# The order in DRAM of the expert weights between two stages of a mixture-of-experts kernel

## What is computed

```python
eidx, gates = ...            # 8 heads x 16 choices out of 128*128 experts, per token
act = gelu(einsum('td,thkd->thk', hb, u_tab[eidx]))
out = einsum('thk,thkd->td', gates * act, v_tab[eidx])
```

## Time and profile before

| | |
|---|---|
| median of 3 runs | 2834.89 us (2833.07 to 2837.03) |
| profiled execution, its own time | 2837.42 us |
| its span | 2835.6 us |
| TensorE clock granted, mean | 0.971 of full speed |
| `weigh` | about 1950 to 2259 us |
| `combine` | 2259 us to the end |
| DMA packets, all queues | 192715, 535.04 MB |

### The profile page before, as it was taken

The page is one execution under the profiler, slowest core; times in us unless marked ns, Lnnn a source line. Parts: engine busy times, 40 slices in busy tenths (PEclk is TensorE's granted clock), DMA queues, the critical chain, the costliest instruction groups (busy, mean ns, idle before and its releaser), DMA issues. The chain is left out here.

```text
span 2835.6 us, 37682 instructions
## 1 busy us (share of the span) xinstructions
PE 2651.7 (94%) x13701; PEld 2227.5 (79%) x13701; DVE 1932.5 (68%) x3068; ACT 1044.9 (37%) x1667; POOL 1293.0 (46%) x607
## 2 busy tenths in 40 slices
PE   8999999799999999889688999999999889999997
PEld 6888877555778887668476899998999868888776
DVE  5445232687754444465755177778999789999999
ACT  4222321355232223222122133335666534444343
POOL 4444442111344444333133457773222267777774
PEclk9999999899999999999798999999999989999999
DMA  5444342112334443222002355557999999999995
GB/s 194 148 148 129 105 152 60 46 59 90 89 119 141 141 154 111 81 90 74 15 7 73 92 150 159 167 166 286 398 377 380 368 346 372 376 375 376 376 372 185
DMA packets 192715, 535.04 MB, mean 189 GB/s; under 512 B 20192, under 2 KB 99296, under 8 KB 172512
## 3 DMA queue, kind: packets, MB, share of 16 engines
q1 hardware_dynamic: 94496, 305.11, 33.5%
q0 software_dynamic: 18432, 134.23, 11.9%
q10 hardware_dynamic: 79680, 94.38, 9.5%
HBM read 478.09 MB, written 55.57 MB: 188 GB/s over the span
## 5 line engine op out<-in xcount | busy, mean ns | idle before, releaser
L352 POOL TENSOR_TENSOR ring_low<-ring,ring_high 128x1024 fp32r<-128x1024 f32 x323 | 801.5, 2485 | 1065.9 <-ACT ring_high L312 1061.9
L403 PE MATMUL ps<-u_high,ring_high 128*128 128x512 f32 (+1 forms) x1728 | 659.3, 382 | 51.9 <-DVE u_low L659 16.9
L404 PE MATMUL ps<-u_low,ring_high 128*128 128x512 f32 (+1 forms) x1728 | 650.4, 376 | 0.0
L405 PE MATMUL ps<-u_high,ring_low 128*128 128x512 f32 (+1 forms) x1728 | 650.3, 376 | 0.0
L312 ACT ACTIVATE ring_high<-ring 128x1024 fp32r<-128x1024 f32 x354 | 373.4, 1055 | 566.0 <-PE ps L405 527.4
L403 PEld LDWEIGHTS ps<-u_high,ring_high 128*128 128x128 f32 x1728 | 328.3, 190 | 114.3 <-issue 40.7
L404 PEld LDWEIGHTS ps<-u_low,ring_high 128*128 128x128 f32 x1728 | 328.7, 190 | 48.8 <-issue 2.0
L405 PEld LDWEIGHTS ps<-u_high,ring_low 128*128 128x128 f32 x1728 | 328.3, 190 | 49.0
L2490 POOL DMA_INDIRECT fetched_rows<-in_peer_uv,fetch_index x128 | 166.2, 1299 | 311.8 <-DVE ps L2510 274.1
L352 POOL TENSOR_TENSOR ring_low_more<-ring,ring_high_more 128x1024 fp32r<-128x1024 f32 x96 | 245.1, 2565 | 32.1 <-ACT ring_high_more L312 31.5
L3088 DVE TENSOR_TENSOR expert_coef_low<-expert_product,expert_coef_high 128x384 fp32r<-128x384 f32 x128 | 216.4, 1691 | 9.3 <-ACT expert_coef_high L3049 9.2
(11 more groups left out here) (439 smaller groups left out, 4865.1 us busy)
## 6 DMA issues: line engine op xcount, KB each, us to landing
ring<-in_peer_u SPq DMA_DIRECT2D x128, 512.0 KB
ring<-in_peer_uv SPq DMA_DIRECT2D x128, 512.0 KB
ring<-in_ffn_gu SPq DMA_DIRECT2D x88, 512.0 KB
ada_weights<-in_ada_w SPq DMA_DIRECT2D x48, 512.0 KB, 4.2
ring<-in_ffn_down SPq DMA_DIRECT2D x48, 512.0 KB
expert_acts<-kept_acts ACTq DMA_DIRECT2D x128, 192.0 KB, 5.0
expert_weights<-weight_stage ACTq DMA_DIRECT2D x24, 1024.0 KB, 10.0
group_acts<-expert_acts ACTq DMA_DIRECT2D x14, 1536.0 KB, 17.8
```

Of the source, the lines that this page charges most:

```text
L352: pool.tensor_tensor(k.lows[p], k.ring[:, s], k.highs[p].bitcast(F32), ALU.subtract)\
L403: pe.matmul(out, k.highs[p][:, w], high, start=first, stop=False)
L404: pe.matmul(out, k.highs[p][:, w], low, start=False, stop=False)
L405: last = pe.matmul(out, k.lows[p][:, w], high, start=False, stop=final)
```

## The change

The intermediate tensor `expert_weights` gets another order in DRAM. Before, it is [block of 16 tokens, partition, expert tile, token]; after, it is [group of eight tiles, partition, block, tile and token]. With it, a store of a block, whose source is one run of 8 KB in each partition, goes to 16 runs of 512 bytes (one in each group; from one group to the next it is 128 x 24 x 512 bytes = 1.5 MiB), 2048 pieces in all instead of 128. The load of a whole group with all 24 blocks, before 24 runs of 512 bytes in each partition (3072 pieces), is one run of 12 KB in each partition (128); for group 1, with 23 blocks, 2944 pieces become 128 runs of 11.5 KB. The two loads of parts of group 0 (two tiles: 128 bytes for each block; six tiles: 384 bytes) keep their 2944 pieces each. Nothing else is changed: the same DMAs, in the same order, with the same waits and the same bytes.

```diff
@@ -2887,8 +2887,8 @@ (weigh, ACT: the store of a block)
                     if part == 1:
                         act.wait_ge(taken[b].sem, taken[b].at(h // 2 + 1))
-                        act.dma_start(k.dram["expert_weights"][h // 2],
-                                      stage[:, slot].rearrange("p e t -> p (e t)")).then_inc(x.staged[slot].sem, 16)
+                        act.dma_start(k.dram["expert_weights"][:, :, h // 2].rearrange("g p n -> p g n"),
+                                      stage[:, slot].rearrange("p (g e) t -> p g (e t)", e=8)).then_inc(x.staged[slot].sem, 16)
@@ -2990,7 +2990,7 @@ (combine: the load of a group)
         def load_weights(eng, g, blocks, lo, hi, landed):
             eng.dma_start(weights[:, g % 2, 0:blocks, lo * WT:hi * WT],
-                          k.dram["expert_weights"][0:blocks, :, 8 * g + lo:8 * g + hi].rearrange("b p e t -> p b (e t)"))\
+                          k.dram["expert_weights"][g, :, 0:blocks, lo * WT:hi * WT])\
                .then_inc(landed.sem, 16)
@@ -3162,7 +3162,7 @@ (build)
-        weights = nc.dram_tensor("expert_weights", (NB, P, P, WT), F32, kind="Internal").ap()
+        weights = nc.dram_tensor("expert_weights", (V_ITERS, P, NB, 8 * WT), F32, kind="Internal").ap()
```

## The result

| | before | after |
|---|---|---|
| median on the same chip | 2833.98 us (2832.33 to 2837.03, 4 runs) | 2858.17 us (2856.26 to 2863.81, 4 runs) |
| ratio | | 1.0084, 95% interval 1.0072 to 1.0096 |
| span of the profiled execution | 2835.6 us | 2854.4 us |
| `weigh`, from DVE's first one-hot to ACT's last activations | 317.5 us | 340.3 us |
| from there to the first product of group 1 | 48.1 us | 47.1 us |

The change costs 24 us. The forecast was 2838 us, a change too small to be measured; 24 us are four times the 5.7 that the prediction calls the least that can be told from none, and 2858 is above its range, which ended at 2856. The table places the loss: 22.8 us in `weigh`, -1.0 in the passage, +0.5 in what follows. (These make 22.3; the profiled spans lie only 18.8 apart because the stages ahead of `weigh`, which the change doesn't touch, ended 3.6 us earlier in that execution.)

What follows compares the result with a forecast made beforehand. Engines were taken to set the pace of weigh and combine, with the DMA close behind. Terms of +4 (ACT's queue), -1 (passage) and 0 (throughput) gave +3 us: a median of 2838 us, forecast's own range 2831 to 2841, overall 2830 to 2856.

Steps and rivals of the forecast that it cites:

- the term of ACT's queue: In weigh, ACT's next DMA is held behind a 2048-piece store: 0.5 us an iteration, +4 us in eight.
- the room that the sum relied on: In weigh, buffers behind ACT's queue absorb 2.4 us of backlog: slots refilled 13.4 us after a store that lands in 9.8.
- Rival (c): In weigh, ACT is held at every store, 24 times 1 to 2 us felt by PE and DVE: about 2862 us; chance 0.12.
- What a piece costs: DMA price: 512-byte pieces move at 294 GB/s, 27.9 ns each, so a megabyte costs 1.4 times that in long pieces.
- weigh's throughput at 0: In weigh, short stores raise DMA demand to 40.4 us against 40.1 an iteration; taken as 0, bounds 0 and +8 us.
- Rival (b): In weigh, DMA becomes the bound if a store's piece costs over 28 ns (33 estimated): 2847 us; chance 0.25.
- (d): In weigh, stores with pieces 1.5 MiB apart run at half rate, +88 us: 2923 us; chance 0.03.
- Combine: In combine, long loads cut DMA work from 32.6 to 31.0 us a group, but nothing waits for DMA: gain 0.
- The passage: Between weigh and combine, group 1's weights load faster but the last stores land later: net -1 us, bounds -4 and +5.
- Rival (e): Long load runs are cut into 512-byte pieces anyway while stores are short, the passage losing its gain: 2841 us; chance 0.03.
- (f): Faster: weigh holds its pace without any hold, and the passage gains its 2 to 4 us and 3 to 4 more: 2828 us; chance 0.11.

Runs made afterwards that it cites:

- e13: The kernel after, with each weight store cut into two halves of eight groups, one issued by ACT and one by SP: 2839.91 us, 1.0012 of before.
- e4: The kernel after, with the 24 weight stores issued by SP between its ring loads instead of by ACT: 2841.89 us, 1.0017 of before.
- e1: The kernel after, with weight stores in long 8 KB runs as before and loads still long (values permuted): 2836.78 us, 0.9996 of before.
- e7: The kernel before, with group 0 loaded in one piece and four ring tiles loaded ahead of group 1 in the passage: 2827.55 us, 0.9975 of before.
- e11: The kernel before, with one more wait: DVE waits at tile 12 of combine for the weights of group 2: 2835.17 us, 0.9999 of before.
- e14: e7 with long stores and long loads of the weights (values permuted): 2831.66 us, 0.9982 of before.
- e5: The kernel after, with the tensor laid out by sixteen tiles, so a store has 1024 pieces of 1 KB: 2847.46 us, 1.0039 of before.
- e10: The kernel after, with weigh's 64 stores of activations issued by SP, the weight stores staying on ACT: 2850.34 us, 1.0047 of before.

## Why the prediction was wrong

**The step that failed is the term of ACT's queue**: +4 us taken, some 20 us measured (22.8 in weigh less the 2.4 that e13 leaves). That is within the term's own bounds, 0 and 3 us an iteration (24 in all); the forecast stood near the lower one. The mechanism was the one described there: a hold of the DMA issued behind a store, until some of its pieces have gone. Four things in the sizing were off.

- When the store starts. "Alone, 35 pieces take 1.0 us and start a little over 1 us after the issue: no hold." No row gave that start. By the packet records it is 3.6 us (median of 24 stores), and ACT's next issue comes 1.4 to 2.7 us behind the store, before it has started in 21 of 24 cases; 36 us of the holds are this.
- How long the other queues keep taking turns. I let one gather and one or two ring tiles (8 packets an engine for each) stand against 35 pieces (3 to 5 us). In the first hold 52 packets of q10 went by, and 32 of the gathers and 28 of the ring took turns with them, 14.35 us in all. The sign of it was in the trace of before (rows below). I had read landing times from 1982 us on the earlier trace rows, that is without the first iteration, which alone lost 13.0 of the 22.8 us.
- What stands behind the held issue. I looked at the next copy of activations, ahead of which ACT idles for 2.72 us. Behind two of three stores it is the copy of a half out of PSUM that stands there (63.0 us of waits at L2885, 25.4 at L2743), and PE's next products into these banks wait for it (26.0 us, 12.7 before).
- How often. "The first two stores of an iteration I cost at nothing; if that cover is gone, they cost the same again": 23 of 24 stores held the issue behind them, not one in three. In six of the eight iterations (all but the second and the fourth) the time grew by 0.8 us or more.

What the second point left unread, the DMA of the kernel before from 1942 to 1982 us: the gathers' queue (42.4% over all of 1942 to 2222), and the landing of the three long stores of that iteration.

```profile
q0 software_dynamic: 1234, 8.96, 53.9%
...
expert_weights<-weight_stage ACTq DMA_DIRECT2D x3, 1024.0 KB, 18.0
```

These stores landed in 18.0 us where later ones do in 9.8: the room that the sum relied on was used up there already.

Of the 112 us of holds a fifth reached the end; a sum over holds would have been as wrong as my 4 us.

**Rival (c)**, at 0.12, was what happened: +24 to +48 by its text, +24.2 measured, by ACT and PE that feel the holds. Only it isn't spread over all stores alike, as that text has it: more than half falls in one iteration.

**What a piece costs** was wrong for the stores. The 27.9 ns are a load's. Where ACT's queue is alone in after, 1981 to 1982.5 us, stored pieces of 512 bytes go by like this:

```profile
DMA packets 1019, 0.52 MB, mean 347 GB/s; under 512 B 1, under 2 KB 1019, under 8 KB 1019
```

These are 1.5 us x 16 / 1019 = 23.6 ns each; two more such stretches of after (2049.8 to 2051, 1990.8 to 1992.6) show 346 and 349 GB/s, and one of e4 on SP's queue (2011 to 2012) 347. The loads of the kernel before stay at 292 (2361.2 to 2362.4). So, with the 410 GB/s of the prediction for long pieces, a stored megabyte in 512-byte pieces costs 410 / 347 = 1.18 times what it costs in long ones, not 1.4. The prediction set the 1.17 of the Trainium skill (DMA: Bandwidth & Descriptors, section Why small descriptors are slow) aside because a trace of loads disagreed with it; the trace of the stores agrees. With 347 the three stores of an iteration cost 1.4 us more, not 3.0, and the demand is 38.8 us in 40.1: under the pace of the engines, not 0.3 over. So **weigh's throughput at 0** came out right (within the 2.4 us that e13 leaves), though the cover for it, room in the buffers, wasn't needed. Rival (b) needed more than 28 ns and is out, and so is (d), which needed twice the price. In (d) the reading of a rule went too far: the Trainium skill (DMA: Bandwidth & Descriptors, section Latency and other measured facts) gives the loss by the pitch from one partition's row to the next. That pitch is 8 KB in the loads of before and 12 KB in the stores of after, and the 1 and 1.5 MiB lie between the pieces of one partition, so neither kernel tests the rule.

That q10 alone falls behind, as the prediction argued, is so, and no slot was waited for. But ACT was held by its queue before any buffer was full, and the argument looked at the buffers.

**Combine** held: 3062 packets in a group (some 3040 forecast), 33.69 us against 33.65, and e1 shows the same without the disturbed start. The demand of the DMA fell, and nobody had waited for it. The 12 KB runs cost the ring nothing: ACT's waits for the ring from 2320 to 2830 us are one of 0.5 us.

**The passage**: -1.0 us measured, net -1 forecast, and in its parts DVE starts later (+2.9 us of wait) and the ring comes sooner (-1.5). The signs are as argued; that the sum meets the forecast is luck, as single executions of the same order of loads lie up to 5 us apart. Rival (e) is out by the packets, (f) by weigh.

## What to carry to other kernels

A relayout that makes one side long makes the other side short; ask which queue gets the short side, and count turns, not bytes. Where three queues have work, a 512-byte piece costs its queue the time of one piece of each of the others (0.43 us here, 18 times its own 0.024), so a transfer cut into 128 pieces an engine is slow and blocks whoever issues next on that queue. Put such pieces on a queue whose engine has nothing urgent to do (e4 lost 0.17%), or on two queues (e13, 0.12%, in place of 0.84%). Take the price of a piece from the direction that you change, loads or stores; and read holds and landing times in the busiest iteration, not in the typical one.

## What was not expected

**Two gaits of combine.** The same instructions run through a group in 33.65 us in before and in 32.4 in e7, which is worth more than everything tried on the layout. VectorE's operations in the kernel before, 2450 to 2750 us (count, busy us, mean ns, idle before):

```profile
L3088 DVE TENSOR_TENSOR expert_coef_low<-expert_product,expert_coef_high 128x384 fp32r<-128x384 f32 x72 | 124.8, 1734 | 0.0
L3102 DVE TENSOR_TENSOR expert_product<-group_acts,group_weights 128x384 f32<-128x384 f32 x72 | 83.9, 1165 | 0.0
```

The same stretch of e7:

```profile
L3110 DVE TENSOR_TENSOR expert_product<-group_acts,group_weights 128x384 f32<-128x384 f32 x74 | 95.1, 1285 | 24.5 <-issue 24.5
L3096 DVE TENSOR_TENSOR expert_coef_low<-expert_product,expert_coef_high 128x384 fp32r<-128x384 f32 x73 | 73.5, 1007 | 5.5 <-ACT expert_coef_high L3057 5.4
```

The subtraction takes 1734 ns in one and 1007 in the other. How that comes is seen in the order of time; DVE in the kernel before:

```profile
2517.89 5.63 DVE L3088 TENSOR_TENSOR expert_coef_low<-expert_product,expert_coef_high 128x384 fp32r<-128x384 f32 x1
```

POOL in the same 6 us:

```profile
2518.35 4.75 POOL L352 TENSOR_TENSOR ring_low_more<-ring,ring_high_more 128x1024 fp32r<-128x1024 f32 x2
```

Here it takes 5.63 us and ends 0.4 us after two subtractions of POOL in a row. Of DVE's subtractions that start in 2450 to 2750 us the 45 that meet none of POOL's take 0.55 us each, the 26 that meet one 3.75 on the mean; in e7 there are 54 and 19, and the 19 take 2.3. The Trainium skill (GPSIMD Engine Reference, section Specifications) says that POOL shares its SBUF interfaces with VectorE and contends with its instructions of two SBUF inputs; this row is such a case. In these 300 us of before DVE is never idle and PE is busy for 49.0 of each 50; in e7 PE is never idle and DVE stands for 30 us. In e7 DVE had to stop for group 1's weights, and the engines went on in another order. e11 forces one such stop by a wait and changes nothing else: its later groups run at 32.6 us, but the stop costs as much as they gain. e14 has no stop and stays at 33.7. How to get the fast gait without a stop wasn't tried. One of e14's eleven executions took 2815.08 us, where the others took 2826 to 2835. That is about what 13 groups at the fast gait and no stop would give, but it wasn't the profiled one, so its cause is open.

**The limit of the queue** at which an issue is held was taken from SP's queue, at about 90 runs an engine. On ACT's queue it can be counted from the runs issued and the packets that have started. In after, when the 24 issues held for more than 1 us came through, 28 to 126 runs an engine were left, 85 in the median, and the most that stood before an issue that wasn't held was 96. The median fits, but the spread is wide: three of these holds ended when under 7 of the store's own runs had started. And nine of the ten holds of e5 began with 41 to 74 runs left (of 1 KB), and two of e10's three with 12 and 36. A fixed number of runs, counted as a mean over the 16 engines, doesn't explain these. What holds an issue in the end stays open.
